# Context products in three rounded passes, seven of eight chunks of two blocks ahead of them, and a wait moved to the user of its bank

## The chip, the cores and the metric

The kernel runs on one core of a Trainium2 chip. The metric is the device time of one execution in microseconds (us). Before the change it is 1469.12 us, the median of three runs (1468.83 to 1469.87).

## The reference

Two transformer layers follow each other on 512 tokens of width 1024, everything in float32. The change lies in the very first projection of the first layer. What is computed there, cut to what matters:

```python
h     = modulate(rms_norm(x, norm1_w),   shift_x,   scale_x)      # 512 tokens
h_ctx = modulate(rms_norm(ctx, norm1_w), shift_ctx, scale_ctx)    # 256 context tokens
p     = h @ w_in          # 1024 -> 3088 columns: q, k, v, z, xs, b, c, dt
p_ctx = h_ctx @ w_in      # of it k, v, xs, b and dt are used
```

Behind it come rotary neighbourhood attention (local keys and all context keys in one softmax), a convolution with SiLU and a chunked state-space scan over context and tokens, the output projection, a gated feed-forward layer, and then the second layer with windowed attention and another feed-forward layer.

## The kernel before, in words

**Matrices.** All activations are kept transposed: features on the 128 partitions, tokens along the free dimension. The weights come in blocks of 128x2048 floats (1 MB). In the input projection a block holds two tiles of 128 output features, each as eight chunks of 128x128 (DC = 8, one for each 128 input features). Tile n belongs to block n // 2, and its product goes to PSUM bank n % 4. KINDS lists the tiles: 0 to 3 are k, 4 to 7 are v, 8 to 11 are xs, 12 and 13 are b, 14 and 15 are c, 16 to 19 are z, 20 to 23 are q.

**Rounded passes.** TensorE takes plain float32, or float32 rounded to a shorter mantissa (F32R). For the 512 tokens each factor is split: `w_hi` is the rounded weight, `w_lo` the rest, `h_hi` and `h_lo` the same of the activations. The product is the sum of three rounded matmuls for each chunk, hi by hi, hi by lo, lo by hi (`chunk_products`, line 267). ScalarE makes `w_hi` by a copy (`high`, line 250), GpSimd makes `w_lo` by a subtraction in four parts (`low`, line 257), and both wait until TensorE is done with the block that used the same buffer two blocks ago (`half_used`). `lo_done` tells TensorE that a block is ready.

**Context.** The 14 tiles 0 to 13 (N_CTX) are also multiplied with the 256 context tokens (`ctx_product`, line 1196). This is done in plain float32: the raw weights by `HC`, the context after its modulation. It goes to banks 4 and 5 in turn, and the second next one waits until the bank is copied out (`ctx_free`). Each plain matmul shows as two records in the trace, each rounded one as a single record. Since TensorE reads the raw weights here, `load_block` (line 241) on the sync engine's queue (SP) waits for `half_used` as well as for `lo_done` before it loads the next block into the same raw buffer. The columns for dt are multiplied separately (lines 1239 to 1243), three rounded passes for the tokens and plain float32 with `HC` for the context.

**Order on TensorE.** `lead` (line 282) starts block 0 while the activations are still being made: chunk k of both tiles as soon as `h_low` says that chunk k is there. Ahead of the last chunk stand the context products 0 and 1. Then follow context 2, tile 2, context 3, tile 3. A small plain product (line 1217) makes the bias row of the second layer's attention in bank 7. TensorE then waits until VectorE has taken it out of that bank (`brow_sb`, line 1258), and goes on with tiles 4 to 22, for each the context product and then the tile (`w_in_tile`, line 1206). Between them stand groups of four transposes (`turn_group`, line 1219), two behind each of the tiles 8 to 13, into banks 6 and 7 in turn, each of which waits until ScalarE has copied an earlier one out (`tr_out`).

**VectorE, by tile** (from line 1885). Tiles 0 to 3: copy the context's bank out, then the rotary embedding of the tile (`rope`, line 1832: one, four and one operations). Behind tile 3 it adds a mask row to the bias row (line 1918). Tiles 4 to 11: the context's result, and two chunks of the modulation of later stages (`add_ada1`, line 1772; chunks 8 to 23, 1 MB each, in a ring of two slots). Tiles 8 to 13: two outer taps of the convolution for the tile and for the context.

**ScalarE, by tile** (from line 1537). It makes the high half of block n // 2 + 2 behind every odd tile, copies the v tiles out, does the centre tap and the SiLU of the convolution, copies the transposes out, and issues the loads of the modulation chunks: chunk 2n + 1 at the head of tile n and chunk 2n + 2 at its end. Each such load waits until VectorE is done with the chunk that had the slot.

**SP** issues the block loads in order. The write of the bias row to DRAM stands between blocks 3 and 4. Behind block 10 come the loads for the bias of the first attention and the copying of the bias row to 128 rows in DRAM.

**GpSimd** makes the low halves in order. Behind block 3 it waits until the bias row is written and sets a part of the arena (A_QT, which later takes q) to zero (line 1120).

**Arena.** Most buffers lie in one arena, by hand-made offsets. X (the normalised tokens, A_X = 13824, 4096 floats long) is dead once `h_hi` and `h_lo` are made. A_QT starts at the same offset, and so does the bias row's small constant buffer (A_CON2) at 15872 within it. A_XST (17920) is first written by tile 8.

Of the kernel before, what the change touches and what calls it, by code (L numbers as in the profile page):

```python
# [6 lines left out]
ALU = mybir.AluOpType  # L7
ACT = mybir.ActivationFunctionType
# [6 lines left out]
DC = D // P  # L15
S = 512
CTX = 256
# [22 lines left out]
N_CTX = 14  # L40
# [24 lines left out]
A_KT, A_KCT, A_X, A_XST, A_BT, A_CT, A_COS, A_SIN, A_TMP = 10752, 12800, 13824, 17920, 19968, 20992, 22016, 22528, 23040  # L65
A_QT, A_ZT, A_CON2 = 13824, 25088, 15872
A_VCTX, A_VKEY, A_DTRAW, A_XTOK, A_BTOK, A_ROW1 = 0, 2048, 1024, 6144, 27136, 27136
# [29 lines left out]
def build(nc, T):  # L97

    es = ExitStack()
    with es:  # L100
# [3 lines left out]
        def sem(name):  # L104
            return es.enter_context(nc.semaphore(name))
# [74 lines left out]
        sq_done, sq_used, mean_done = sem("sq_done"), sem("sq_used"), sem("mean_done")  # L180
        xn_done, aff_done, h_low, hctx_ready = sem("xn_done"), sem("aff_done"), sem("h_low"), sem("hctx_ready")
        tap_done, tap_silu = sem("tap_done"), sem("tap_silu")
# [37 lines left out]


        aside = {b: (over[:, at:at + BLK], over[:, at + BLK:at + 2 * BLK]) for b, at in A_ASIDE.items()}

# [16 lines left out]

        def load_block(sp, b, off=0, wait_pe=False):

            if b >= 2 or not isinstance(off, int):
                sp.wait_ge(lo_done, (b - 1) + off)
                if wait_pe:
                    sp.wait_ge(half_used, 2 * (b - 1))
            src = T["w"][bass.ds(b + off, 1)].rearrange("a p n -> p (a n)")
            sp.dma_start(w_raw[b % 2][:], src).then_inc(raw_in[b % 2], 16)
# [32 lines left out]

        def lead(pe, b, h_from, ctx_product=None, between=None):


            pe.wait_ge(lo_done, b + 1)
            for k in range(DC):
                if k == DC - 1 and ctx_product:
                    ctx_product(0)
                    ctx_product(1)
                pe.wait_ge(h_low, h_from + k + 1)  # L290
                for ft in (0, 1):
                    last = chunk_products(b, ft, ps[ft], k)
                    if k == DC - 1:
                        last.then_inc(half_used, 1)
            if between:
                between()
            pe.wait_ge(lo_done, b + 2)
            for ft in (0, 1):
                if ctx_product:
                    ctx_product(2 + ft)  # L300
                for k in range(DC):
                    last = chunk_products(b + 1, ft, ps[2 + ft], k)
                last.then_inc(half_used, 1)
# [731 lines left out]
        def _(sp):  # L1035
# [19 lines left out]
            sp.dma_start(arena[0:32, A_CON2:A_CON2 + 1024], T["con2"]).then_inc(con2_in, 16)  # L1055
            load_block(sp, 2, wait_pe=True)
            load_block(sp, 3, wait_pe=True)
            sp.wait_ge(brow_sb, 1)
            sp.dma_start(brow_dram, brow).then_inc(brow_out, 16)
            for b in range(4, 11):  # L1060
                load_block(sp, b, wait_pe=b - 2 < 7)
            sp.wait_ge(ada_used, 24)
# [47 lines left out]
        def _(pool):  # L1110
# [7 lines left out]
            lows(2, 2)  # L1118
            pool.wait_ge(brow_out, 16)
            nc.gpsimd.memset(A(A_QT, 4096), 0.0).then_inc(at1["zero"], 1)  # L1120
            lows(4, B_OUT - 4)
            low(pool, B_OUT)
# [47 lines left out]
        def _(pe):  # L1170
# [25 lines left out]
            def ctx_product(n, off=0):  # L1196
                raw = w_raw[(n // 2) % 2][:, :].rearrange("p (f k n) -> p f k n", f=2, k=DC)
                if n >= 2:
                    pe.wait_ge(ctx_free, n - 1 + off)
                for k in range(DC):  # L1200
                    if n == 0:
                        pe.wait_ge(hctx_ready, k + 1)
                    last = nc.tensor.matmul(ps[4 + n % 2][:, 0:CTX], raw[:, n % 2, k, :], HC[:, k, :], start=k == 0, stop=k == DC - 1)  # L1203
                last.then_inc(ctx_done, 1)
# [8 lines left out]

            lead(pe, 0, 0, ctx_product, lambda: pe.wait_ge(row1_out, 2))

# [3 lines left out]
            def turn_group(k):  # L1219
                if k >= 2:  # L1220
                    pe.wait_ge(tr_out, k - 1)
                if k == 0:
                    pe.wait_ge(tile_free, 8)
                if k == 8:
                    pe.wait_ge(tap_silu, TAPS_OF_XS)
                if k == 12:
                    pe.wait_ge(dt_act, 1)
                if k == 16:
                    pe.wait_ge(tap_silu, TAPS_OF_BCT)
                for m, src in enumerate(TR[k][0]):  # L1230
                    last = nc.tensor.transpose(ps[6 + k % 2][:, m * 128:(m + 1) * 128], src, ident)
                last.then_inc(tr_done, 1)
# [24 lines left out]

            pe.wait_ge(brow_sb, 1)
            for n in range(4, 23):
# [246 lines left out]
        def _(act):  # L1506
# [25 lines left out]
            act.wait_ge(hctx_scaled, 1)  # L1532
            for c in range(DC):
                nc.scalar.activation(HC[:, c, :], HC[:, c, :], ACT.Identity, bias=mod1[:, c, 1:2],
                                     scale=gain1[:, c, 1:2]).then_inc(hctx_ready, 1)
            taps = 0
            for n, (kind, j) in enumerate(KINDS):
                if n == 5:
                    load_ada(act, T["ada1"][10], 10)
                if 5 <= n < 12:  # L1540
                    load_ada(act, T["ada1"][2 * n + 1], 2 * n + 1)
                if kind in ("xs", "b", "c"):
                    m = {"xs": 0, "b": 4, "c": 6}[kind] + j
                    todo = [({"xs": xsT, "b": bT, "c": cT}[kind], ps[n % 4][:, :], tmp[:, 2, :], half_used, tile_free)]
                    if n < N_CTX:
                        todo.append(({"xs": xscT, "b": bcT}[kind], ps[4 + n % 2][:, 0:CTX], tmp[:, 3, 0:CTX], ctx_done, ctx_free))
                    for dst, src, buf, made, summed in todo:
                        act.wait_ge(made, n + 1)
                        if taps:
                            act.wait_ge(tap_silu, taps)  # L1550
                        taps += 1
                        nc.scalar.activation(buf, src, ACT.Identity, bias=conv[:, 3, m:m + 1],
                                             scale=conv[:, 1, m:m + 1]).then_inc(tap_done, 1)
                        act.wait_ge(summed, n + 1)
                        nc.scalar.activation(dst[:, j, :], buf, ACT.Silu).then_inc(tap_silu, 1)
# [213 lines left out]
        def _(dve):  # L1769
# [47 lines left out]
            for c in range(DC):  # L1817
# [5 lines left out]
                if c in (3, 5):  # L1823
                    k = (c - 3) // 2
                    dve.wait_ge(row1_done, 1)
                    nc.vector.tensor_copy(row1[:, 512 * k:512 * k + 512], ps[2 + k][:, :]).then_inc(row1_out, 1)
            dve.wait_ge(wdt_h, 1)
            nc.vector.tensor_tensor(wdt_lo[:], wdt[:], wdt_hi[:], ALU.subtract).then_inc(wdt_ready, 1)
# [391 lines left out]
```

## Time and profile before

| what | value |
|---|---|
| median of three runs | 1469.12 us |
| the profiled execution, its own time | 1470.08 us |
| its span, first to last instruction | 1468.3 us |
| TensorE busy | 1376.2 us (94%) |
| VectorE, ScalarE, GpSimd busy | 572.7, 583.6, 626.0 us |
| mean granted TensorE clock | 0.969 of full speed |

The span is the stretch that the trace covers; what the execution took beyond it, 1.8 us, lies around it. PE is TensorE's matmuls, PEld its weight loads, DVE is VectorE, ACT is ScalarE, POOL is GpSimd, SPq and ACTq the issuing of DMAs. A busy PE is not a PE at its peak: the duration of one matmul (some 390 ns) holds its way through the array, while the next one starts 216 to 230 ns later. The pace is read from a group's length over its count. Times within the trace are from the start of the span.

### The profile page before, as it was taken

To read this page: it belongs to the slowest core of one execution; us is meant where nothing else is said; L and a number is where in the kernel's file an instruction comes from. 1 tells how busy PE (TensorE), PEld (TensorE's weight loads), DVE (VectorE), ACT (ScalarE), POOL (GpSimd) and SP (SyncE) were. 2 spreads that over 40 slices of the span, in tenths; PEclk is the share of its full clock that TensorE was granted. 3 is DMA by queue.
4 is the path that set the end of the run, shared out by engine and by line. 5 is a ranking of instruction groups with operands and counts; after the bars stand their busy time and mean duration, and the time that the engine had idled before them with its cause. 6 is when DMAs were issued, how large, how long until landed. Compare 5 with 4: busy or idle time off the path is not lost.

```text
span 1468.3 us, 17191 instructions
## 1 busy us (share of the span) xinstructions
PE 1376.2 (94%) x6306; PEld 1099.9 (75%) x6306; DVE 572.7 (39%) x1080; ACT 583.6 (40%) x897; POOL 626.0 (43%) x516
## 2 busy tenths in 40 slices
PE   8989999896788799999999989899979999999997
PEld 1778878785676688888888878655768888888885
DVE  2655623677823634444334352467060000001113
ACT  3513444672312544344322443477353322322331
POOL 0232324337614354444465754333514454454563
PEclk9999999999889899999999989999989999999999
DMA  9226575000013244554433322200201322222221
GB/s 393 101 87 244 215 185 180 6 30 1 1 58 143 86 191 181 202 198 171 172 144 114 137 93 86 86 1 1 87 29 58 114 86 93 107 86 96 105 86 58
DMA packets 26984, 165.55 MB, mean 113 GB/s; under 512 B 2688, under 2 KB 4992, under 8 KB 8496
## 3 DMA queue, kind: packets, MB, share of 16 engines
q1 hardware_dynamic: 24912, 150.11, 28.1%
q10 hardware_dynamic: 2016, 14.68, 2.6%
q8 instruction: 36, 0.59, 0.2%
q14 instruction: 20, 0.16, 0.0%
HBM read 162.65 MB, written 6.32 MB: 115 GB/s over the span
## 4 chain that ended last, share of the span: by engine, by line
PE 84%; POOL 5%; DVE 4%; ACT 3%; issue 2%; DMA 1%; SPq 0%; ACTq 0%; DVEq 0%; POOLq 0%
PE bank L271 51%; PE bank L335 9%; PE bank L312 5%; PE bank L1203 3%; PE bank L668 2%; PE bank L648 2%; PE bank L521 2%; POOL arena L846 1%; POOL w_lo L264 1%; PE bank L1176 1%; DMA w_raw<-w_dram 1%; PE bank L510 1%; POOL arena L848 1%; PE bank L658 1%; PE bank L498 1%
## 5 line engine op out<-in xcount | busy, mean ns | idle before, releaser
L264 POOL TENSOR_TENSOR w_lo<-w_raw,w_hi 128x512 fp32r<-128x512 f32 x352 | 471.3, 1370 | 652.9 <-ACT w_hi L255 652.9
L271 PE MATMUL bank<-h_hi,w_hi 128*128 128x512 f32 x1120 | 445.4, 398 | 16.0 <-POOL w_lo L264 8.1
L271 PE MATMUL bank<-h_lo,w_hi 128*128 128x512 f32 x1120 | 439.7, 393 | 0.0
L271 PE MATMUL bank<-h_hi,w_lo 128*128 128x512 f32 x1120 | 439.6, 392 | 0.0
L255 ACT ACTIVATE w_hi<-w_raw 128x2048 fp32r<-128x2048 f32 x89 | 170.5, 1916 | 365.9 <-PE bank L271 189.6
L271 PEld LDWEIGHTS bank<-h_hi,w_hi 128*128 128x128 f32 x1120 | 213.0, 190 | 61.7 <-issue 13.7
L271 PEld LDWEIGHTS bank<-h_hi,w_lo 128*128 128x128 f32 x1120 | 212.6, 190 | 45.3
L271 PEld LDWEIGHTS bank<-h_lo,w_hi 128*128 128x128 f32 x1120 | 212.9, 190 | 43.6
L2081 DVE TENSOR_TENSOR arena<-arena,bank 128x512 f32 (+1 forms) x22 | 15.1, 688 | 210.2 <-PE bank L271 210.2
L1953 DVE TENSOR_TENSOR h_lo<-arena,h_hi 128x1024 fp32r<-128x1024 f32 x22 | 32.7, 1502 | 136.9 <-ACT h_hi L1630 125.4
L1797 DVE SCALAR_TENSOR_TENSOR arena<-bank,params,arena 128x511 f32<-128x511 f32 (+1 forms) x36 | 25.4, 705 | 140.6 <-ACT arena L1610 114.6
L335 PE MATMUL bank<-w_hi,h_hi 128*128 128x512 f32 x192 | 75.0, 391 | 4.7 <-POOL arena_rounded L232 3.3
L335 PE MATMUL bank<-w_hi,h_lo 128*128 128x512 f32 x192 | 75.1, 391 | 0.0
L335 PE MATMUL bank<-w_lo,h_hi 128*128 128x512 f32 x192 | 74.9, 390 | 0.0
L1788 DVE CUSTOM_DVE_ANT_0 ada_ring<-ada_ring,arena 128x1024 f32<-128x1024 f32 x48 | 62.1, 1331 | 0.0
L1203 PE MATMUL bank<-arena,w_raw 128*128 128x256 f32 x224 | 53.0, 392 | 4.1 <-DVE arena L1918 4.1
L804 POOL TENSOR_SCALAR arena<-arena,small 128x256 f32<-128x256 f32 (+1 forms) x64 | 32.8, 531 | 55.6 <-DVE small L762 55.6
L1203 PEld LDWEIGHTS bank<-arena,w_raw 128*128 128x128 f32 x224 | 43.8, 198 | 11.4 <-DVE arena L1918 5.0
L648 PE MATMUL bank<-arena 128*128 128x256 f32 (+1 forms) x128 | 44.1, 458 | 3.5 <-DVE ada_ring L2037 2.6
L1778 DVE CUSTOM_DVE_ANT_0 ada_ring<-ada_ring,arena,params 128x1024 f32<-128x1024 f32 x32 | 42.3, 1368 | 10.6 <-DMA ada_ring<-ada_dram 10.6
L335 PEld LDWEIGHTS bank<-w_hi,h_hi 128*128 128x128 f32 x192 | 36.2, 188 | 13.4 <-issue 3.7
L616 POOL TENSOR_SCALAR arena<-arena,small 128x512 f32<-128x512 f32 x32 | 21.8, 692 | 51.6 <-DVE small L595 51.6
(263 smaller groups left out, 1859.4 us busy)
## 6 DMA issues: line engine op xcount, KB each, us to landing
w_raw<-w_dram SPq DMA_DIRECT2D x92, 1024.0 KB, 4.8
ada_ring<-ada_dram SPq DMA_DIRECT2D x30, 1024.0 KB, 4.8
ada_ring<-ada_dram ACTq DMA_DIRECT2D x14, 1024.0 KB, 5.2
arena<-ada_dram SPq DMA_DIRECT2D x4, 1024.0 KB, 9.7
arena<-x_dram SPq DMA_DIRECT2D x2, 2048.0 KB, 11.7
bias_copies<-bias_rows SPq DMA_DIRECT2D x1, 4096.0 KB, 28.0
arena<-bias_copies SPq DMA_DIRECT2D x1, 3072.0 KB, 14.7
out_dram<-arena SPq DMA_DIRECT2D x8, 256.0 KB, 2.1
```

What stands on the lines that cost most here:

```text
L255: nc.scalar.activation(w_hi[b % 2][:], w_raw[b % 2][:], ACT.Copy).then_inc(hi_done, 1)
L264: last = nc.gpsimd.tensor_tensor(w_lo[b % 2][:, part], w_raw[b % 2][:, part], w_hi[b % 2][:, part], ALU.subtract)
L271: last = nc.tensor.matmul(bank[:, :], w[:, ft, k, :], x[:, k, :], start=k == first and m == 0, stop=k == final and m == 2)
L312: last = nc.tensor.matmul(ps[f][:, :], w[:, k, f, :], x[:, 2 * gslot + k, :], start=bank_free is not None and k == 0 and m == 0, stop=False)
L335: last = nc.tensor.matmul(ps[2 * t + h][:, :], x[:, slot + k, part], w[n][:, k, cols], start=start and m == 0, stop=stop and m == 2)
L521: last = nc.tensor.matmul(ps[7][:, 0:256], v, pt1[G % 2][:, kb, :], start=kb == 0, stop=kb == 3)
L648: nc.tensor.matmul(ps[u % 3][:, 0:128 * (hi - lo)], q2[:, 2 * g + hq // 2, t * 128:(t + 1) * 128], k2[:, g, hq % 2, lo * 128:hi * 128], st ...
L804: nc.gpsimd.tensor_scalar(prob2[:, u % 8, 0:w], prob2[:, u % 8, 0:w], row_inv[:, u % 16:u % 16 + 1], 1.0, ALU.mult, ALU.mult).then_inc(s[" ...
L1203: last = nc.tensor.matmul(ps[4 + n % 2][:, 0:CTX], raw[:, n % 2, k, :], HC[:, k, :], start=k == 0, stop=k == DC - 1)
L1778: last = nc.vector.tensor_tensor_reduce(out=src, in0=src, in1=row1, scale=1.0, scalar=par_("adab")[:, 16 + at:17 + at], op0=ALU.mult, op1= ...
L1788: last = nc.vector.tensor_tensor_reduce(out=src, in0=src, in1=row2, scale=1.0, scalar=0.0, op0=ALU.mult, op1=ALU.add, accum_out=dots[:, 2 ...
L1953: nc.vector.tensor_tensor(h_lo[:, slot:slot + 2, :], HID[:, chunk, :], h_hi[:, slot:slot + 2, :], ALU.subtract)\
```

## The change

- `ctx_product` multiplies `w_hi` and `w_lo` with `hc_hi` and `hc_lo` in three rounded passes: 24 matmuls of 256 columns in place of 8 plain ones.
- ScalarE makes `hc_hi` (rounded) beside `HC`, which stays in place for dt: 16 activations for 8. VectorE makes `hc_lo` in four subtractions, of two chunks each. Both new tensors lie where X was (A_HCH = 13824), and the constants of the bias row move to 17920.
- TensorE no longer reads the raw weights, so `load_block` waits for `lo_done` alone.
- `lead` is written out for these two blocks: chunks 0 to 6 of block 0, then chunks 0 to 6 of block 1, then context 0 and 1, the last chunk of tiles 0 and 1, context 2, the last chunk of tile 2, context 3, the last chunk of tile 3.
- TensorE's wait for `brow_sb` moves from ahead of tile 4 to turn group 0, behind tile 8.
- GpSimd's zeroing moves behind block 7 and waits for the last context product. ScalarE waits ahead of tile 8 until the bias row is written to DRAM.

```diff
@@
-A_QT, A_ZT, A_CON2 = 13824, 25088, 15872
+A_QT, A_ZT, A_CON2, A_HCH = 13824, 25088, 17920, 13824
@@
+        hc_hi, hc_lo = view(over, A_HCH - A_OVER, DC, CTX), view(over, A_HCH - A_OVER + DC * CTX, DC, CTX)
@@
-        def load_block(sp, b, off=0, wait_pe=False):
+        def load_block(sp, b, off=0):
...
                 sp.wait_ge(lo_done, (b - 1) + off)
-                if wait_pe:
-                    sp.wait_ge(half_used, 2 * (b - 1))
@@
-            load_block(sp, 2, wait_pe=True)
-            load_block(sp, 3, wait_pe=True)
+            load_block(sp, 2)
+            load_block(sp, 3)
             sp.wait_ge(brow_sb, 1)
             sp.dma_start(brow_dram, brow).then_inc(brow_out, 16)
             for b in range(4, 11):
-                load_block(sp, b, wait_pe=b - 2 < 7)
+                load_block(sp, b)
@@
             lows(2, 2)
-            pool.wait_ge(brow_out, 16)
+            lows(4, 4)
+            pool.wait_ge(ctx_done, N_CTX)
             nc.gpsimd.memset(A(A_QT, 4096), 0.0).then_inc(at1["zero"], 1)
-            lows(4, B_OUT - 4)
+            lows(8, B_OUT - 8)
@@
             def ctx_product(n, off=0):
-                raw = w_raw[(n // 2) % 2][:, :].rearrange("p (f k n) -> p f k n", f=2, k=DC)
+                hi, lo = (w[(n // 2) % 2][:, :].rearrange("p (f k n) -> p f k n", f=2, k=DC) for w in (w_hi, w_lo))
                 if n >= 2:
                     pe.wait_ge(ctx_free, n - 1 + off)
                 for k in range(DC):
-                    if n == 0:
-                        pe.wait_ge(hctx_ready, k + 1)
-                    last = nc.tensor.matmul(ps[4 + n % 2][:, 0:CTX], raw[:, n % 2, k, :], HC[:, k, :], start=k == 0, stop=k == DC - 1)
+                    if n == 0 and k % 2 == 0:
+                        pe.wait_ge(hctx_low, k // 2 + 1)
+                    for m, (w, x) in enumerate(((hi, hc_hi), (hi, hc_lo), (lo, hc_hi))):
+                        last = nc.tensor.matmul(ps[4 + n % 2][:, 0:CTX], w[:, n % 2, k, :], x[:, k, :], start=k == 0 and m == 0, stop=k == DC - 1 and m == 2)
                 last.then_inc(ctx_done, 1)
@@
-            lead(pe, 0, 0, ctx_product, lambda: pe.wait_ge(row1_out, 2))
+            pe.wait_ge(lo_done, 1)
+            for k in range(DC - 1):
+                pe.wait_ge(h_low, k + 1)
+                for ft in (0, 1):
+                    chunk_products(0, ft, ps[ft], k)
+            pe.wait_ge(row1_out, 2)
+            pe.wait_ge(lo_done, 2)
+            for ft in (0, 1):
+                for k in range(DC - 1):
+                    chunk_products(1, ft, ps[2 + ft], k)
+            pe.wait_ge(h_low, DC)
+            ctx_product(0)
+            ctx_product(1)
+            for ft in (0, 1):
+                chunk_products(0, ft, ps[ft], DC - 1).then_inc(half_used, 1)
+            for ft in (0, 1):
+                ctx_product(2 + ft)
+                chunk_products(1, ft, ps[2 + ft], DC - 1).then_inc(half_used, 1)
@@
                 if k == 0:
                     pe.wait_ge(tile_free, 8)
+                    pe.wait_ge(brow_sb, 1)
@@
-            pe.wait_ge(brow_sb, 1)
             for n in range(4, 23):
@@
             for c in range(DC):
+                nc.scalar.activation(hc_hi[:, c, :], HC[:, c, :], ACT.Identity, bias=mod1[:, c, 1:2], scale=gain1[:, c, 1:2]).then_inc(hctx_high, 1)
+                act.wait_ge(hctx_high, 2 * c + 1)
                 nc.scalar.activation(HC[:, c, :], HC[:, c, :], ACT.Identity, bias=mod1[:, c, 1:2],
-                                     scale=gain1[:, c, 1:2]).then_inc(hctx_ready, 1)
+                                     scale=gain1[:, c, 1:2]).then_inc(hctx_high, 1)
@@
+                if n == 8:
+                    act.wait_ge(brow_out, 16)
@@
+            for c in range(0, DC, 2):
+                dve.wait_ge(hctx_high, 2 * c + 4)
+                nc.vector.tensor_tensor(hc_lo[:, c:c + 2, :], HC[:, c:c + 2, :], hc_hi[:, c:c + 2, :], ALU.subtract).then_inc(hctx_low, 1)
             dve.wait_ge(wdt_h, 1)
```

## Rows read from the trace of the kernel before

**Rows 1.** The page: span, busy time, and the group of the modulation chunks.
```profile
span 1468.3 us, 17191 instructions
...
PE 1376.2 (94%) x6306; PEld 1099.9 (75%) x6306; DVE 572.7 (39%) x1080; ACT 583.6 (40%) x897; POOL 626.0 (43%) x516
...
L1778 DVE CUSTOM_DVE_ANT_0 ada_ring<-ada_ring,arena,params 128x1024 f32<-128x1024 f32 x32 | 42.3, 1368 | 10.6 <-DMA ada_ring<-ada_dram 10.6
```

**Rows 2.** Chain of waits, 60 to 110 us: start, length, engine, line, count.
```profile
74.91 3.45 PE bank L1203 x16
78.36 5.47 PE bank L271 x24
83.85 0.69 DVE arena L1836
...
88.10 0.69 DVE arena L1918
88.83 6.17 PE bank L1203 x16
...
103.93 5.45 PE bank L271 x24
109.38 3.45 PE bank L1203 x16
```

**Rows 3.** Windows 80 to 100 us: busy time, then granted clock, DMA share, GB/s.
```profile
80.00:90.00 10.00, 5.94 (x22) 3.91 (x21) 4.91 (x8) 0.65 (x1) 0.00 (x0) 0.85 0.32 109
90.00:100.00 10.00, 10.00 (x38) 8.17 (x37) 4.96 (x8) 1.26 (x1) 8.42 (x5) 0.81 0.00 0
```

**Rows 4.** Chain of waits further on: transposes, tiles 14 and 15, dt.
```profile
136.10 0.87 PE bank L1231 x8
...
186.01 10.92 PE bank L271 x48
196.93 5.51 PE bank L1240 x24
```

**Rows 5.** Groups by form, weight loads: busy and mean ns of one, idle before.
```profile
L271 PEld LDWEIGHTS bank<-h_hi,w_hi 128*128 128x128 f32 x1120 | 213.0, 190 | 61.7 <-issue 13.7 <-POOL w_lo L264 2.6 <-DVE h_lo L1819 2.0
...
L1231 PEld LDWEIGHTS bank<-constants,arena 128*128 128x128 f32 x76 | 8.9, 140 | 1.3
```

**Rows 6.** Timeline, 55 to 100 us: start, length, engine, line, what, idle before.
```profile
55.75 4.03 ACT L1534 ACTIVATE arena<-arena,small 128x256 f32<-128x256 f32 x8
...
57.56 7.07 PE L1203 MATMUL bank<-arena,w_raw 128*128 128x256 f32 x32
...
65.36 0.69 DVE L1836 SCALAR_TENSOR_TENSOR arena<-bank,arena 128x512 f32<-128x512 f32 x1 [3.61 <-PE bank L271]
...
66.06 2.79 DVE L1840 SCALAR_TENSOR_TENSOR arena<-bank,arena 32x512 f32<-32x512 f32 x4
...
69.61 0.42 DVE L1896 TENSOR_SCALAR arena<-bank 128x256 f32<-128x256 f32 x1
...
69.95 0.68 DVE L1836 SCALAR_TENSOR_TENSOR arena<-bank,arena 128x512 f32<-128x512 f32 x1
...
71.23 1.92 ACT L255 ACTIVATE w_hi<-w_raw 128x2048 fp32r<-128x2048 f32 x1 [11.45 <-DMA w_raw<-w_dram]
...
73.22 5.43 POOL L264 TENSOR_TENSOR w_lo<-w_raw,w_hi 128x512 fp32r<-128x512 f32 x4 [26.02 <-ACT w_hi L255]
...
73.47 1.60 DVE L1843 TENSOR_TENSOR arena<-arena 128x512 f32<-128x512 f32 x1
...
96.23 3.52 POOL L1120 MEMSET arena<- 128x4096 f32 x1
```

**Rows 7.** Timeline of ScalarE, centre taps of tiles 8, 9 and 11.
```profile
136.28 0.76 ACT L1552 ACTIVATE arena<-bank,params 128x512 f32<-128x512 f32 x1
...
146.69 0.78 ACT L1552 ACTIVATE arena<-bank,params 128x512 f32<-128x512 f32 x1 [4.19 <-DVE small L1778]
...
167.18 0.78 ACT L1552 ACTIVATE arena<-bank,params 128x512 f32<-128x512 f32 x1 [3.87 <-DVE small L1778]
```

More of the change, by code:

```diff
@@ L180, in build @@
         sq_done, sq_used, mean_done = sem("sq_done"), sem("sq_used"), sem("mean_done")
-        xn_done, aff_done, h_low, hctx_ready = sem("xn_done"), sem("aff_done"), sem("h_low"), sem("hctx_ready")
+        xn_done, aff_done, h_low = sem("xn_done"), sem("aff_done"), sem("h_low")
+        hctx_high, hctx_low = sem("hctx_high"), sem("hctx_low")
         tap_done, tap_silu = sem("tap_done"), sem("tap_silu")
@@ L280, in products, with lead @@
             last.then_inc(half_used, 1)
-        def lead(pe, b, h_from, ctx_product=None, between=None):
+        def lead(pe, b, h_from, between=None):
             pe.wait_ge(lo_done, b + 1)
             for k in range(DC):
-                if k == DC - 1 and ctx_product:
-                    ctx_product(0)
-                    ctx_product(1)
                 pe.wait_ge(h_low, h_from + k + 1)
@@ L298, in lead @@
             for ft in (0, 1):
-                if ctx_product:
-                    ctx_product(2 + ft)
                 for k in range(DC):
```

## The prediction

> **What bounds the kernel now.** The page first: TensorE is busy 1376.2 of 1468.3 us [rows 1]. The change touches the input projection only (57 to 186 us), so there I read the chain of waits. It runs on TensorE almost alone: per tile 3.45 us of context product (16 records, line 1203) and 5.45 us of three-pass product (24 records, line 271) [rows 2]. One hole stands out: tile 3 ends at 83.83, TensorE then waits for VectorE (rotation of tile 3, then the bias row of line 1918), and the context product that starts at 88.83 takes 6.17 us, not 3.45 [rows 2]; the granted clock of those stretches is 0.85 and 0.81 [rows 3], which is time spent at 1.2 instead of 2.4 GHz after the idle stretch. From 95 to 186 TensorE waits for nobody. So what is taken from TensorE here comes off the end, as long as no other engine sets the pace.
>
> **Context products, 14 of them.** Before: 3.45 us each. After: 24 rounded matmuls of 256 columns, a form that no row shows. A plain record of 256 columns takes 3.45/16 = 216 ns, one of 128 columns 0.87/8 = 109 ns [rows 2, 4]: 107 ns per 128 columns, at two passes over each. A rounded matmul of 512 columns takes 10.92/48 = 227.5 ns [rows 4]: one pass over 512 columns (4 x 53.4 = 214) and 14 ns more. The 14 isn't the weight load: with 16 weight columns instead of 128 it is 5.51/24 = 230 ns [rows 4]. I take it as fixed: 107 + 14 = 120.6 ns, so 2.89 us a product and 0.56 x 14 = **7.8 us saved**. Bounds: 109 ns (the 128-column record, no surcharge), and 190 ns, the recorded length of one weight load [rows 5], if loads didn't overlap the stream. I sit near the low end, since the 128-column records follow at 109 ns although each loads 128 weight columns for 140 ns on average [rows 5].
> The Trainium skill ("TensorE: Matmul & The Clock Gate", Back-to-back issue gap) gives N/2.4 + 2.5 ns, 109 ns at 256 columns; by it the sum below would be 3.9 us larger. At 512 columns it says 216 where the row has 227.5, so I hold to the row.
>
> **The bias row's wait.** From 83.83 to 95.00 are 11.17 us, in which the context product (3.45) and the bias product of line 1217 (two plain records of 512 columns, 4 x 216 ns = 0.86) are all the work there is: 6.86 us of idling and of slow clock go. **6.9 saved.** The wait now stands ahead of turn group 0, behind tile 8, over 25 us after the row is made (line 1918 then ends near 94): free. It moves nothing else on TensorE's queue but tiles 4 to 8. On SP, the bias row's DMA and the loads of blocks 4 and on still stand behind it; block 4 is needed only at tile 8. ScalarE's new wait on that DMA (before tile 8) and the copies that follow on SP come no earlier or later than their users.
>
> **The lead.** 42 products of block 1 go ahead of the context: 57.56 + 42 x 0.2275 = 67.1. Behind them the rounding of the context has to be ready. ScalarE's eight activations take 4.03 us [rows 6]; sixteen, alternating with waits on its own results, 8 to 9.5, so to 65.3; VectorE's four differences (0.7 each) trail by one, 66. Hidden with 1 us to spare; without the lead it would cost some 8 us. What is late next: tiles 0 to 3 now end within 9 us of each other, and VectorE needs 4.6 us for each (start of one rotation to the next, 65.36 to 69.95, the context's copy included [rows 6]). TensorE: context 0 to 70.0, context 1 to 72.9, the last chunks of tiles 0 and 1 to 73.6 and 74.3, context 2 to 77.2, tile 2 to 77.9. Context 3 needs its bank's copy, which stands behind the rotation of tile 0: 73.8 + 4.25 + 0.4 = 78.4. The last step of a rotation took 1.60 instead of 0.69 us beside GpSimd's subtraction [rows 6], and block 2's subtraction now lies there (its high half at 74.5 to 76.4, then 5.4 us): 79.3. **1.5 us lost.** Then context 3 to 82.2, tile 3 to 82.9, bias product to 83.8, by which time the copy for context 4 is made (79.2 + 4.6) and block 2's low half too (81.8). Tile 5 ends at 100.5, where it ended at 109.4 [rows 2].
>
> **Weight loads and GpSimd.** Blocks 2 and 3 load at 57 instead of behind TensorE's last use of the raw block (ScalarE's idle time ahead of block 2's high half was a DMA's, 11.45 us [rows 6]); now only the freed w_hi gates them, which isn't on TensorE's path. The 3.52 us memset [rows 6] waits for context 13 and then lies beside tile 13's product (5.46 us), before the subtraction of block 8, which waits for that product's end anyway: 0.
>
> **The other loop.** In tiles 8 to 11 ScalarE waits at each tile's head for VectorE's modulation chunks, to issue the next load, before it may start the convolution's tap: the taps stand (167.18 - 136.28)/3 = 10.3 us apart [rows 7], while TensorE's period with two turn groups was 9.8 and becomes 9.2. The lag grows by 1.1 us a tile. From where it starts: tile 8 ends at 126, tap 8 at once, if chunk 15 is done by then. VectorE is free for chunk 8 at 93.5; a pair of chunks takes 5.5 us of work (4 x 1.37 [rows 1]) and, by the loads (some 5 us each, two slots), about 8 us: chunk 15 is done at 123, just in time. Taps then at 126, 136.5, 147, 157; their context results 4.7 us behind, turned tiles copied 6.2 behind. Context 13 asks for 162 at 163.8; turn groups 9 to 11 wait a few tenths each: **0.6 lost**.
> Behind tile 13 every wait hangs on TensorE's own progress: the shift reaches the end whole.
>
> **The sum.** 7.8 + 6.9 - 1.5 - 0.6 = 12.6 us. The profiled execution took 1470.08 (its span 1468.3); it would take 1457.5. The median of the runs is 1469.1, 1.0 below that: **1456.5 us**. 0.2% (3 us) is about what a measurement of this kernel can tell from no change.
>
> **Rivals.**
> A, no surcharge: 256 rounded columns cost 109 ns, as the 128-column records do. 24 x 0.109 = 2.61, 3.9 us more: 1452.6. For: nothing in the 14 ns says that it doesn't scale with columns. Against: it would have to vanish rather than halve. The page's gap rule, named above, would give this.
> B, the modulation loop takes over: if the chunks start late (blocks 4 and 5 load at the same time as chunks 10 and 11), the lag stands at tile 9 already and TensorE goes at 10.3 instead of 9.2 through five tiles: 5.5 us given back, 1462.0. For: its spare is under 3 us. Against: two tiles of slack in the banks.
> C, three loads for two: the passes cost together what the plain ones did (144 ns each): only 4.8 us stay, 1464.3.
> D, slower: the weight load of a rounded pass isn't hidden behind only 256 columns, and 190 ns [rows 5] is the step: 24 x 0.19 = 4.56, 1.11 x 14 = 15.5 lost against 4.8 won: 1479.8. It decides from 158 ns a matmul on. Against: 109 ns in rows 4. The same page (What overlaps and what doesn't) says that loads overlap running matmuls only in other row groups, which would make D likely; the 227.5 ns at 512 columns leaves no room for a load in series, so the trace disagrees.
>
> **Chances.** Forecast 0.60, A 0.13, B 0.10, C 0.09, D 0.05; 0.03 for a gain that is absorbed further on. Range 1451.5 (A with fewer stalls) to 1464.5 (C). Faster 0.92, same 0.03, slower 0.05.
>
> **What would show it.** 24 records in about 2.9 us for a context product; no hole at 84 to 89 and clock 1.0 from 60 to 200; a wait of 1 to 2 us ahead of context 3, released by VectorE; tile 6 beginning near 100.5; ScalarE's taps 10.3 apart and TensorE's tiles 9.2; the products of tiles 14 and 15 beginning near 173.4 where they began at 186.0 [rows 4]. Wrong would make it: a step of over 140 ns, or TensorE waiting for VectorE between tiles 9 and 13.

## The result, and the profile after

The changed kernel takes 1460.62 us (median of 4 runs, 1458.23 to 1460.96), beside 1468.97 us before (4 runs): 8.35 us or 0.57% faster, the ratio 0.9938 with a 95% interval of 0.9921 to 0.9956. The forecast was 1456.5 us, with a range of 1451.5 to 1464.5. Sign and range were right, and a third of the forecast gain is missing. The measured time lies 4.1 us above the forecast and 1.4 us below rival B, the modulation loop, which had 1462.0 and a chance of 0.10.

The page of the changed kernel, its span, its busy times and its chain by engine:

```profile
span 1459.0 us, 17423 instructions
...
PE 1367.3 (94%) x6418; PEld 1095.5 (75%) x6418; DVE 580.0 (40%) x1084; ACT 588.1 (40%) x905; POOL 634.3 (43%) x516
...
PE 77%; DVE 9%; POOL 5%; ACT 4%; issue 3%; DMA 3%; ACTq 0%; SPq 0%; DVEq 0%; POOLq 0%
```

TensorE's share of the chain is 77%; VectorE has 9% and DMAs have 3%. The chain of waits from 67 us on, where it used to be almost TensorE's alone [rows 2], shows where that comes from (start, length, engine, line):

```profile
67.25 5.76 PE bank L1200 x48
73.02 0.71 PE bank L271 x3
...
93.51 1.19 DVE ada_ring L1796
94.71 1.20 DVE ada_ring L1796
95.95 7.66 DMA ada_ring<-ada_dram
103.63 1.28 DVE ada_ring L1796
104.92 2.22 DVE ada_ring L1796
107.18 5.05 DMA ada_ring<-ada_dram
...
115.08 7.38 DMA ada_ring<-ada_dram
...
130.93 0.79 ACT arena L1570
...
178.85 10.93 PE bank L271 x48
189.78 5.50 PE bank L1255 x24
```

The first line has the price that no row of the kernel before showed: two context products, 48 rounded matmuls of 256 columns, in 5.76 us, **120 ns each**. From 73.75 on the chain has left TensorE. It goes through VectorE's rotations, the modulation chunks (line 1796) and the loads of the next chunks, into ScalarE's tap of tile 8, and on through the same loop. It comes back to TensorE only with the last group of transposes, at 177.71, and the products of tiles 14 and 15, which begin at 178.85. They began at 186.01 [rows 4] and were forecast near 173.4.

The windows that answer to [rows 3] (busy time of PE, PEld, DVE, ACT, POOL, then granted clock, DMA share, GB/s):

```profile
80.00:90.00 10.00, 10.00 (x62) 8.14 (x61) 9.74 (x16) 1.92 (x1) 7.19 (x6) 1.00 0.01 2
90.00:100.00 10.00, 10.00 (x57) 8.75 (x56) 8.57 (x15) 1.21 (x4) 0.29 (x1) 1.00 0.55 199
```

The hole is gone, and with it the slow stretch behind it: the granted clock is 1.00 (2.4 GHz) where it was 0.85 and 0.81. The taps of tiles 8 to 11 on ScalarE, which answer to [rows 7]:

```profile
130.93 0.78 ACT L1570 ACTIVATE arena<-bank,params 128x512 f32<-128x512 f32 x1 [8.46 <-DVE small L1796]
...
141.04 0.78 ACT L1570 ACTIVATE arena<-bank,params 128x512 f32<-128x512 f32 x1 [3.86 <-DVE small L1796]
...
152.16 0.78 ACT L1570 ACTIVATE arena<-bank,params 128x512 f32<-128x512 f32 x1 [3.08 <-DVE small L1796]
...
162.26 0.78 ACT L1570 ACTIVATE arena<-bank,params 128x512 f32<-128x512 f32 x1 [3.86 <-DVE small L1796]
```

The distance is (162.26 - 130.93)/3 = 10.4 us, where it was 10.3. Tile 8's tap comes at 130.93, not at 126 as forecast. TensorE notices through the transposes, not through the context's banks. These are its waits between 56 and 190 us (who, released by whom, in total, times, longest):

```profile
PE bank L1246 <- ACT arena L1607: 4.7, 4, 1.9
PE bank L1200 <- DVE arena L1917: 0.9, 1, 0.9
```

### The profile page after: what moved, and what is told of

The parts are those of the page before. It is cut to its first block, busy times and chain, and to the rows that moved or that the text cites. A ratio compares the mean times of both kernels' runs of the same rounds, so it can differ in the third digit from the quotient of the medians.

```text
span 1459.0 us, 17423 instructions
## 1 busy us (share of the span) xinstructions
PE 1367.3 (94%) x6418; PEld 1095.5 (75%) x6418; DVE 580.0 (40%) x1084; ACT 588.1 (40%) x905; POOL 634.3 (43%) x516
## 4 chain that ended last, share of the span: by engine, by line
PE 77%; DVE 9%; POOL 5%; ACT 4%; issue 3%; DMA 3%; ACTq 0%; SPq 0%; DVEq 0%; POOLq 0%
PE bank L271 47%; PE bank L330 10%; PE bank L307 5%; DVE ada_ring L1796 2%; PE bank L663 2%; PE bank L643 2%; PE bank L516 2%; DMA ada_ring<-ada_dram 2%; POOL arena L841 1%; PE bank L1172 1%; POOL w_lo L264 1%; DMA w_raw<-w_dram 1%; PE bank L505 1%; POOL arena L843 1%; PE bank L653 1%
## 5 line engine op out<-in xcount | busy, mean ns | idle before, releaser
L264 POOL TENSOR_TENSOR w_lo<-w_raw,w_hi 128x512 fp32r<-128x512 f32 x352 | 479.3, 1393 | 635.1 <-ACT w_hi L255 635.1
L271 PE MATMUL bank<-h_hi,w_hi 128*128 128x512 f32 x1120 | 442.2, 395 | 14.1 <-POOL w_lo L264 7.1
L271 PE MATMUL bank<-h_hi,w_lo 128*128 128x512 f32 x1120 | 438.7, 392 | 0.0
L1796 DVE CUSTOM_DVE_ANT_0 ada_ring<-ada_ring,arena,params 128x1024 f32<-128x1024 f32 x32 | 47.7, 1542 | 9.9 <-DMA ada_ring<-ada_dram 9.9
L307 PE MATMUL bank<-h_hi,w_hi 128*128 128x512 f32 x112 | 43.7, 390 | 0.0
L307 PE MATMUL bank<-h_hi,w_lo 128*128 128x512 f32 x112 | 43.6, 389 | 0.0
```

What stands on the lines that cost most here:

```text
L264: last = nc.gpsimd.tensor_tensor(w_lo[b % 2][:, part], w_raw[b % 2][:, part], w_hi[b % 2][:, part], ALU.subtract)
L271: last = nc.tensor.matmul(bank[:, :], w[:, ft, k, :], x[:, k, :], start=k == first and m == 0, stop=k == final and m == 2)
L307: last = nc.tensor.matmul(ps[f][:, :], w[:, k, f, :], x[:, 2 * gslot + k, :], start=bank_free is not None and k == 0 and m == 0, stop=False)
L1796: last = nc.vector.tensor_tensor_reduce(out=src, in0=src, in1=row1, scale=1.0, scalar=par_("adab")[:, 16 + at:17 + at], op0=ALU.mult, op1= ...
```

## The experiments

All runs are compared with runs of the kernel before on the same chip. The working theory, called the loop theory in the expectations: from tile 4 on the pace is set by a loop of VectorE's modulation chunks, the loads that each of them releases, and ScalarE's tap, which waits at a tile's head until it has issued such a load. The rival is the one behind the forecast's sum: TensorE's own time sets the pace, and what is missing lies elsewhere. The moment at which tiles 14 and 15 begin is taken from each profile. It is a finer gauge than the total, which has a spread of some us of its own: the four times of one kernel below (both starts) lie up to 5.5 us apart.

### One part alone: the wait moved

```diff
-            pe.wait_ge(brow_sb, 1)
             for n in range(4, 23):
...
                     pe.wait_ge(tile_free, 8)
+                    pe.wait_ge(brow_sb, 1)
```

(in the kernel before)

> The kernel before, with TensorE's wait for the bias row moved to turn group 0 and nothing else. Term of the forecast: 6.9 us, so 1462.1, the hole at 84 to 89 gone and the products of tiles 14 and 15 beginning at 179.1 instead of 186.0. Loop theory (from tile 8 on the loop of VectorE's modulation chunks, their loads and ScalarE's taps sets the pace at some 10.3 us a tile): TensorE's own period stays 9.8 here, the loop begins some 6 us earlier with TensorE, so nearly the same, 1462 to 1464. If the wait alone gives as much as the whole change measured (8.35 us), the three passes gave nothing.

Measured: 1462.09 us, ratio 0.9943 (0.9926 to 0.9959), 6.9 us less than before. Its chain of waits has the products of tiles 14 and 15 at

```profile
179.20 10.92 PE bank L271 x48
```

186.01 - 179.20 = 6.81, where the forecast's term was 6.86. So this term was right, and this one moved line is worth nearly all that the whole change brought. The three passes, the lead and the freed loads together add 0.35 us to that start (179.20 - 178.85), where the sum had 5.7. The medians differ by 1.5 us, but their intervals (0.9926 to 0.9959 and 0.9921 to 0.9956) overlap, so the totals show no difference.

### Loop made shorter: half of each chunk left out

```diff
-                    last = nc.vector.tensor_tensor_reduce(out=src, in0=src, in1=row1, ...
+                    src = src[:, 0:512]
+                    last = nc.vector.tensor_tensor_reduce(out=src, in0=src, in1=row1[:, 0:512], ...
```

(in the changed kernel, as all that follow; half of each modulation dot product is left out)

> The changed kernel with half the columns of each modulation chunk multiplied (512 of 1024; the other half of these dot products is left out), loads and waits as they are. Loop theory: VectorE needs some 2.3 us less a tile, the loop falls under TensorE's 9.2 us, the taps follow TensorE, and the 12.6 us of the forecast appear: 1456.5, tiles 14 and 15 beginning near 173.5. Rival (what was missing lies in TensorE's own work or in later stages): no change from the changed kernel, 1460.6, tiles 14 and 15 at 178.9.

Measured: 1453.85 us, ratio 0.9888 (0.9871 to 0.9904). ScalarE's taps, and then the chain at tiles 14 and 15:

```profile
126.27 0.78 ACT L1570 ACTIVATE arena<-bank,params 128x512 f32<-128x512 f32 x1 [5.95 <-DVE small L1797]
...
134.92 0.78 ACT L1570 ACTIVATE arena<-bank,params 128x512 f32<-128x512 f32 x1 [2.40 <-PE bank L271]
...
144.13 0.78 ACT L1570 ACTIVATE arena<-bank,params 128x512 f32<-128x512 f32 x1 [1.18 <-PE bank L271]
```

```profile
172.59 10.92 PE bank L271 x48
```

From tile 9 on the taps are released by TensorE and stand 9.2 us apart, the period that the forecast gave to TensorE. The start is 0.8 us ahead of the forecast's 173.4. So what was missing lay in the loop.

### Loop started earlier, by its loads

```diff
             load_block(sp, 3)
+            load_block(sp, 4)
+            load_block(sp, 5)
             sp.wait_ge(brow_sb, 1)
...
-            for b in range(4, 11):
+            for b in range(6, 11):
```

> The changed kernel with the loads of blocks 4 and 5 ahead of the bias row's wait on the SP queue, so that they don't run beside chunks 10 and 11. Loop theory: chunk 10 lands some 5 us after its issue instead of 7.7 and the loop begins 2.5 us earlier, 1458. Rival (the loads aren't what delays the loop, the port shared with GpSimd is): chunk 10 lands earlier but tile 8's tap moves by less than 1 us, 1460.

Measured: 1456.12 us, ratio 0.9908 (0.9892 to 0.9925), against 1460.62 for the changed kernel. Its VectorE timeline has chunk 10 (and, under it, the taps and the chain):

```profile
101.23 1.28 DVE L1798 CUSTOM_DVE_ANT_0 ada_ring<-ada_ring,arena,params 128x1024 f32<-128x1024 f32 x1 [2.25 <-DMA ada_ring<-ada_dram]
```

```profile
126.80 0.78 ACT L1572 ACTIVATE arena<-bank,params 128x512 f32<-128x512 f32 x1 [6.13 <-DVE small L1798]
...
136.91 0.78 ACT L1572 ACTIVATE arena<-bank,params 128x512 f32<-128x512 f32 x1 [3.86 <-DVE small L1798]
```

```profile
174.71 10.93 PE bank L271 x48
```

Chunk 10 comes 2.4 us earlier than in the changed kernel (103.63), as expected. Tile 8's tap comes 4.1 us earlier, more than expected. The rest is won at chunks 14 and 15. Chunk 14 begins 3.1 us earlier (119.36 against 122.49), its load having taken 6.23 us from issue to landing instead of 7.38. And of the four operations of chunks 14 and 15 two, not three, fall beside GpSimd's subtraction for block 5, which is 1.0 us. (Block 4's subtraction slows three operations in both kernels, here the last one of chunk 11 and both of chunk 12.) The timelines of VectorE and of GpSimd in the changed kernel show the price of one such meeting:

```profile
103.63 1.28 DVE L1796 CUSTOM_DVE_ANT_0 ada_ring<-ada_ring,arena,params 128x1024 f32<-128x1024 f32 x1 [4.97 <-DMA ada_ring<-ada_dram]
...
104.84 2.30 DVE L1796 CUSTOM_DVE_ANT_0 ada_ring<-ada_ring,arena,params 128x1024 f32<-128x1024 f32 x1
...
107.07 2.30 DVE L1796 CUSTOM_DVE_ANT_0 ada_ring<-ada_ring,arena,params 128x1024 f32<-128x1024 f32 x1
...
109.30 2.29 DVE L1796 CUSTOM_DVE_ANT_0 ada_ring<-ada_ring,arena,params 128x1024 f32<-128x1024 f32 x1
```

```profile
103.76 9.00 POOL L264 TENSOR_TENSOR w_lo<-w_raw,w_hi 128x512 fp32r<-128x512 f32 x4 [13.47 <-ACT w_hi L255]
```

An operation that takes 1.28 us alone takes 2.30, and GpSimd's four parts take 9.00 where they took 5.43 [rows 6]. The Trainium skill ("SBUF — State Buffer", Who interferes with whom) says that a VectorE instruction with both inputs in SBUF and a GpSimd instruction that reads SBUF keep each other out. The trace agrees: each of the two is longer by about 1 us, beside the other only. The two causes, this and the sharing of the DMA engines by several loads, were not moved one at a time. By the trace 3.1 of the 4.1 us are won ahead of chunk 14, 2.4 of them at chunk 10's load, and 1.0 at the meeting.

### Loop started earlier, by its chunks

```diff
+            dve.wait_ge(row1_out, 2)
+            add_ada1(8)
+            add_ada1(9)
             dve.wait_ge(wdt_h, 1)
...
-                if 4 <= n < 12:
-                    add_ada1(2 * n)
-                    add_ada1(2 * n + 1)
+                if 4 <= n < 11:
+                    add_ada1(2 * n + 2)
+                    add_ada1(2 * n + 3)
```

(ScalarE issues the loads of the later chunks one tile earlier to match)

> The changed kernel with modulation chunks 8 and 9 handled by VectorE in its idle stretch ahead of tile 0's rotation (66 to 71 us) and each later pair one tile earlier, their loads too. Loop theory: the loop is one tile ahead, tap 8 follows TensorE at 126, and nearly the whole forecast appears, 1455.5 to 1457. Rival (something else is missing): 1460.6 as the changed kernel.

Measured: 1460.76 us, ratio 0.9940 (0.9923 to 0.9956). A miss of the expectation. The first pair is done by 70.4, but the second still waits for its place behind tile 3's rotation. It releases the third pair's loads at the same moment as ever, together with blocks 4 and 5, and tile 8's tap stands at 130.29. Being a pair ahead doesn't help a loop whose turns begin at the same moment; it only ends one turn sooner. Tiles 14 and 15 begin at 176.86, 2.0 us earlier, and those 2 us are not in the total: the stretch from the first attention to the end took 2 us longer in this profile (1458.9 - 255.95 = 1202.95 us against 1459.0 - 257.96 = 1201.0).

### The lead undone

```diff
-            for ft in (0, 1):
-                for k in range(DC - 1):
-                    chunk_products(1, ft, ps[2 + ft], k)
-            pe.wait_ge(h_low, DC)
...
```

(context 0 and 1 ahead of block 0's last chunk, context 2 and 3 ahead of whole tiles, as in the kernel before)

> The changed kernel with the context products 0 to 3 back at the places that the kernel before gave them (0 and 1 ahead of the last chunk of block 0, 2 and 3 ahead of their tiles), still in three passes. TensorE then waits for the rounded context: context 0 ends near 66.3 instead of 70, tile 4 begins near 88 instead of 84, 4.4 us later. Loop theory (the stretch is paced by VectorE's chunks, which begin when VectorE is through with tile 3's rotation and the bias row): that moment is hardly later, since tiles 0 to 2 end earlier, so the lead is worth about nothing, 1460.6. Rival (TensorE's own time counts): 4.4 us slower, 1465.

Measured: 1462.27 us, ratio 0.9957 (0.9940 to 0.9974). That is 1.65 us above the changed kernel. The two intervals overlap, but tiles 14 and 15 begin 1.6 us later too (180.47). TensorE waits 4.3 us for the rounded context and then runs partly at 1.2 GHz (granted clock 0.66 from 60 to 70 us). The bias row is made 2.2 us later (94.73 for 92.50), and so is the first chunk. Yet chunk 15 is done at 130.2, no later than in the changed kernel (130.4): up to there four of its operations meet GpSimd's subtractions, in the changed kernel six. What holds tile 8's tap is TensorE:

```profile
132.56 0.78 ACT L1569 ACTIVATE arena<-bank,params 128x512 f32<-128x512 f32 x1 [5.42 <-PE bank L271]
```

The tap comes 1.6 us later than in the changed kernel. TensorE itself is 6.8 us later there (it begins the transposes behind tile 8 at 132.31 instead of 125.48). In the changed kernel it had been 5.2 us ahead of the loop, and of its loss only what exceeds these 5.2 us counts. Both theories miss this: the loop theory's zero leaves TensorE out, the rival's 4.4 leaves out the 5.2.

### The wait put back

```diff
+            pe.wait_ge(brow_sb, 1)
             for n in range(4, 23):
...
-                    pe.wait_ge(brow_sb, 1)
```

> The changed kernel with TensorE's wait for the bias row back ahead of tile 4. The row is made at 93.2 there, TensorE idles from 83.8 on, 9.4 us, and some 2.5 us more go at half clock. Loop theory: what counts is the first modulation chunk, which waits for context 4's copy: it moves from 93.4 to some 99.5, 6 us, so 1466.6. Rival (TensorE's own time counts): 12 us slower, 1472.

Measured: 1464.30 us (9 runs), ratio 0.9972 (0.9962 to 0.9982), 3.7 slower than the changed kernel. The longest of TensorE's waits:

```profile
PE bank L1200 <- DVE arena L1939: 9.5, 1, 9.5
```

TensorE idles for 9.5 us and gets a granted clock of 0.63 between 90 and 100 us. Of those 12 us, 6.2 remain at tiles 14 and 15 (185.07). The rival's 12 is not met. The loop theory's 6 is, but not for its reason: chunk 15 is done at 135.0, 4.6 us later than in the changed kernel, and tile 8's tap, 6.2 us later (137.15), is again released by TensorE. TensorE lost more than the 5.2 us that it had been ahead. The median shows only 3.7 us of it; the single times go from 1463.96 to 1467.52, and the profiled execution is the slowest of them.

### Both starts

Both edits of the two experiments on the loop's start together.

> The changed kernel with both edits of the last call: the loads of blocks 4 and 5 ahead of the bias row, and chunks 8 and 9 early with each later pair one tile earlier. Loads first alone began tiles 14 and 15 at 174.7, chunks early alone at 176.9 instead of 178.9. If they act on different turns of the loop they add: 172.7, the forecast's 173.4 and better, 1454. If one hides the other: 1456, as loads first alone.

Measured: 1456.36 us, ratio 0.9923 (0.9905 to 0.9941), the four times at 1453.85, 1454.21, 1458.52 and 1459.35. Tiles 14 and 15 begin at 173.91, against 174.71 with the loads first alone. They overlap rather than add.

### The three passes undone

```diff
-                    for m, (w, x) in enumerate(((hi, hc_hi), (hi, hc_lo), (lo, hc_hi))):
-                        last = nc.tensor.matmul(ps[4 + n % 2][:, 0:CTX], w[:, n % 2, k, :], x[:, k, :], ...
+                    last = nc.tensor.matmul(ps[4 + n % 2][:, 0:CTX], raw[:, n % 2, k, :], HC[:, k, :], ...
```

(and `load_block` waits until the context products have read the raw block)

> The changed kernel with the 14 context products plain again (raw weights by HC, one matmul of two records a chunk), everything else as changed, the rounding of the context included though unused; block loads wait for the context products of the raw block. TensorE's work grows by 14 x 0.57 = 8 us. Loop theory: what comes behind the start of the chunks (tiles 4 to 13) is hidden under the loop, and only the four products ahead of it count, 2.3 us: 1463. Rival: all of it counts, 1468.6.

Measured: 1462.31 us (5 runs), ratio 0.9958 (0.9944 to 0.9972), 1.7 us above the changed kernel, with overlapping intervals. Tiles 14 and 15 begin 3.8 us later (182.66). The rival's 1468.6 is out. TensorE's eight extra us take the place of idle time: its only wait is 1.5 us for block 2, whose load now waits for TensorE, with a granted clock of 0.87 from 80 to 90 us around it. With no other wait TensorE sets the pace of the whole stretch. It releases the taps of tiles 8 and 9 (132.85, 1.9 us later than in the changed kernel, and 142.96); those of tiles 10 and 11 are released by VectorE (164.16 for tile 11, also 1.9 later). So the three passes are worth at most 3.8 us at tiles 14 and 15 beside this loop, the waiting for block 2 included, and not the 7.8 of the sum.

### The loop's turn made shorter: a version that beats both

```diff
-                if 5 <= n < 12:
+                if 5 <= n < 8:
                     load_ada(act, T["ada1"][2 * n + 1], 2 * n + 1)
...
                         nc.scalar.activation(buf, src, ACT.Identity, bias=conv[:, 3, m:m + 1],
                                              scale=conv[:, 1, m:m + 1]).then_inc(tap_done, 1)
+                        if dst is xsT:
+                            load_ada(act, T["ada1"][2 * n + 1], 2 * n + 1)
```

(on top of the loads first)

> Loads first (blocks 4 and 5 ahead of the bias row), and ScalarE's load of chunk 2n + 1 in tiles 8 to 11 stands behind the tile's centre tap instead of ahead of it. Loop theory: in each turn VectorE idles 1.4 us between its last chunk and its taps, since ScalarE issues the load first and only then taps; with the tap made ahead, a turn falls from 10.3 to some 8.9 us, under TensorE's 9.2, and the taps follow TensorE. Tiles 14 and 15 begin near 173 instead of 174.7: 1454.5. Rival (a turn is bounded by the loads' own way, 5 us and more from issue to landing): turns stay near 10.3, and the later issue makes it 0 to 1 us slower than loads first, 1456 to 1457.

Measured: **1453.38 us** (1452.9 to 1454.51), ratio 0.9895 (0.9876 to 0.9914). The taps, and the chain at tiles 14 and 15:

```profile
126.16 0.78 ACT L1572 ACTIVATE arena<-bank,params 128x512 f32<-128x512 f32 x1 [5.42 <-PE bank L271]
...
135.31 0.78 ACT L1572 ACTIVATE arena<-bank,params 128x512 f32<-128x512 f32 x1 [1.87 <-PE bank L271]
...
144.52 0.78 ACT L1572 ACTIVATE arena<-bank,params 128x512 f32<-128x512 f32 x1 [0.64 <-PE bank L271]
...
153.73 0.78 ACT L1572 ACTIVATE arena<-bank,params 128x512 f32<-128x512 f32 x1 [2.01 <-PE bank L271]
```

```profile
172.98 10.92 PE bank L271 x48
```

Every tap is released by TensorE and they stand (153.73 - 126.16)/3 = 9.2 us apart, with nothing left out of the computation. Between 56 and 190 us TensorE's only wait is the 0.9 us ahead of context 3. The stretch is TensorE's again, and the start of tiles 14 and 15 lies 13.0 us ahead of the kernel before. It lies 1.7 us ahead of the loads first alone; the totals of these two (0.9876 to 0.9914 and 0.9892 to 0.9925) don't differ clearly, while both are clear of the kernel before.

### The three passes alone

Both moves undone, the lead and the wait.

> The changed kernel with both of its moves undone: context products 0 to 3 at their old places and the wait for the bias row ahead of tile 4. Three passes, the rounding of the context and the loads without TensorE's wait are left. TensorE's arithmetic: 8 us fewer, 4 to 6 us more at the start for the rounded context, so 1465 to 1467. Loop theory: the bias row is made at 94.7 as with the old lead, later than the 88.8 of the kernel before; context 4 follows at half clock, its copy and the first chunk at about 100 instead of 95.4, so the loop starts later than before and the kernel is slower than before or equal, 1469 to 1471.

Measured: 1468.60 us (12 runs), beside 1470.07 before on that chip, ratio 0.9995 (0.9985 to 1.0005): no difference. TensorE's waits between 56 and 190 us:

```profile
PE bank L1200 <- DVE arena_rounded L1846: 5.1, 4, 1.3
PE bank L1200 <- DVE arena L1938: 4.9, 1, 4.9
```

The first chunk starts at 100.48, 5.1 us later than before, and tiles 14 and 15 at 187.05, 1.0 later than before. Eight us less work on TensorE, and nothing of it in the time. Some 5 of them lie ahead of tile 8's end. The waits for the rounded context and for the bias row and the slow clock (0.83 from 60 to 70 us, 0.66 from 90 to 100) took these 5 and 2.8 more, beyond what the kernel before lost there: TensorE releases tile 8's tap at 139.12, where it stood at 136.28 [rows 7]. Chunk 15 is done at 136.4, so it isn't the loop's start that decides here. Behind the tap 1.8 us come back. The expectation's sign was right in the trace, not in the total, which shows neither gain nor loss.

**The runs read together.** The same moments from each trace (us): when VectorE is done with chunk 15, when ScalarE makes tile 8's tap, and when tiles 14 and 15 begin.

| kernel | chunk 15 done | tap of tile 8 | released by | tiles 14 and 15 | from the tap to there |
|---|---|---|---|---|---|
| changed | 130.4 | 130.93 | VectorE | 178.85 | 47.9 |
| loads first | 126.3 | 126.80 | VectorE | 174.71 | 47.9 |
| lead undone | 130.2 | 132.56 | TensorE | 180.47 | 47.9 |
| wait put back | 135.0 | 137.15 | TensorE | 185.07 | 47.9 |
| three passes alone | 136.4 | 139.12 | TensorE | 187.05 | 47.9 |

In these five, tile 8's tap comes at the later of two moments: when TensorE is done with tile 8, and half a microsecond after chunk 15. From there on it takes 47.9 us, whichever of the two released the tap. It took 49.7 us in the kernel before (136.28 to 186.01) and 46.8 with the loop's turn shortened (tap first, 126.16 to 172.98). So of the 2.9 us that the passes take from TensorE behind tile 8, the loop lets 1.8 through. This is the working theory, put more sharply than the expectations had it: ahead of tile 8 a gain on TensorE counts only while TensorE is the later one there, and behind it only as far as the loop's turn allows.

## Why the prediction was right or wrong

- **The price of a rounded matmul of 256 columns**: 120.6 ns forecast, 120 measured. The surcharge is 13 ns here and 13.5 at 512 columns, so it is fixed, as forecast. Rivals A (109), C (144) and D (190) are out, and with A the N/2.4 + 2.5 ns of the Trainium skill ("TensorE: Matmul & The Clock Gate", Back-to-back issue gap) for this form. Nor do loads and streams run in series, as D had it: each weight load is recorded with 188 ns, and the matmuls follow at 120. The Trainium skill ("TensorE: Matmul & The Clock Gate", What overlaps and what doesn't) has loads overlap only in other row groups; the trace disagrees.
- **The bias row's wait**: 6.86 forecast, 6.81 (tiles 14 and 15) and 6.9 (medians) measured by itself. No slow clock follows: the granted clock is 1.00 from 60 to 200 us.
- **The lead's cost**: 1.5 us forecast ahead of context 3, 0.9 measured. The rotation's last step was longer by 0.37 us beside GpSimd, not by 0.9. The rounding was ready at 65.6, as forecast (66).
- **Weight loads and the memset**: the memset was free, as forecast. The loads were not. The forecast named blocks 4 and 5 beside chunks 10 and 11 only as a reason for rival B. In its own sum they cost nothing because TensorE doesn't need block 4 before tile 8. But the chunks' loads, which they delay, stand in the loop.
- **The step that failed** is "a pair of chunks takes 5.5 us of work and, by the loads, about 8 us: chunk 15 is done at 123, just in time". It was done at 130.4. The pairs began at 93.4, 103.6, 112.3 and 122.5, so 10.2, 8.6 and 10.2 us apart instead of 8, and the last one took 8.0 us of work instead of 5.5. Chunk 10's load took 7.66 us (4.9, from 96.3 to 101.2, with the loads moved) and chunk 14's 7.38 us, issued 2.3 us behind block 6's. The operations beside GpSimd's subtraction took 2.30 us instead of 1.37. I had charged that very effect to the rotation, from one row [rows 6], and not to the chunks, which have both inputs in SBUF too. VectorE's timeline of the kernel before has it at chunk 12:

```profile
118.98 2.09 DVE L1778 CUSTOM_DVE_ANT_0 ada_ring<-ada_ring,arena,params 128x1024 f32<-128x1024 f32 x1 [5.69 <-DMA ada_ring<-ada_dram]
...
121.01 2.29 DVE L1778 CUSTOM_DVE_ANT_0 ada_ring<-ada_ring,arena,params 128x1024 f32<-128x1024 f32 x1
```

  The same timeline has chunk 8 begin at 95.38 and chunk 15 end at 133.1, 37.7 us later. The forecast gave the same eight chunks 29.5 us; they took 37.0.
- **What the step cost**: tap 8 came five us late, and the term "0.6 lost" became 5.9 us (178.85 against 172.98 with the loop shortened). Of it 4.7 are the recorded waits ahead of the transposes. Such a wait is counted from the recorded end of the matmul before it, some 390 ns after its start, where the next one would have started after 227; that is part of the remaining 1.2. Nothing else in that stretch is missing: with the loop shortened, in two ways, TensorE's forecast of 173.4 is met (172.59 and 172.98).
- **Rival B is what happened.** Blocks 4 and 5 loaded beside chunks 10 and 11, TensorE went at (168.05 - 136.74)/3 = 10.4 us a tile, and tiles 14 and 15 began 5.45 us later than forecast, where B had 5.5. The sign named for a wrong forecast, TensorE waiting for VectorE between tiles 9 and 13, came too, by way of ScalarE: its copy of the transposes stands behind a tap that waits for VectorE's chunks. B deserved more than 0.10.
- **Which term went**: the three passes' 7.8. They shorten TensorE in a stretch in which, once the wait was gone, TensorE was no longer the later of two. By itself the moved wait brings 6.9, and the passes, with the rounding that they need and the freed loads, nothing.
- **The total**: at tiles 14 and 15 the changed kernel is 7.2 us ahead of the kernel before, and the medians differ by 8.35. The rest arises in later stages that the change doesn't touch. From the first attention product to the end the profiles took 1203.2 (before), 1201.0 (changed), 1202.8 (wait alone), 1200.7 (loads first) and 1199.0 us (tap first). The earlier start doesn't explain it: with the lead undone that stretch began at 259.56 and took 1199.0, with the chunks early it began at 255.95 and took 1202.95. Its cause stays open, and it caps the accuracy of any sum here at 2 to 4 us. So 1.2 us of the measured gain come from no term of the forecast. They are luck: they brought the time nearer to a forecast that the changed stretch itself missed by 5.45 us.

## What to carry to other kernels

When the busiest engine is shortened in a stretch, write down the period of the next loop beside it (here 10.3 us against 9.8, to become 9.2), and then where that loop starts; a loop that is slower per turn is hidden only until its head start is used up. An engine's queue that issues loads is part of such a loop: letting the tap go ahead of the load brought tiles 14 and 15 forward by 1.7 us (174.71 to 172.98), where the three passes by themselves had moved them 1.0 us back. When a wait is taken away, look at which transfers are now issued together with which others.

## What the runs showed of the hardware

- A float32 matmul with rounded operands costs 120 ns at 256 columns and 227.5 ns at 512, 13 to 14 ns above one pass over the columns at the plain records' rate in both cases; three of them (360 ns) beat one plain product of 256 columns (431 ns).
- VectorE's chunk operation over two SBUF inputs went from 1.28 to 2.30 us beside GpSimd's subtraction. With half the columns it went from 0.75 to 1.78, so the delay is about 1.0 us for each instruction, whatever its length, and not a share of its work.
- The load of a modulation chunk (1 MB) landed 4.9 us after its issue with the blocks' loads moved away, and 7.66 us after it with two more loads of 1 MB in flight. In that time the DMA engines were busy throughout (share 0.99 to 1.02, 414 to 434 GB/s from 97 to 105 us).
